# Nine of twelve convolution panels by seven block products, gated attention kept in DRAM meanwhile, and row tile loads held behind the first weights

## What is computed

```python
h = rms_norm(x, g_mix); z = h @ w_in
q, k, v, r, a_lr, c_b, c_c, c_x, g_a, g_b = split_columns(z)
o = gla_chunked(q, k, v, log_a)                 # 4 heads
o = rms_norm(o, g_gla) * silu(r)                # "gated attention"
y_a = o @ w_branch_a
y_conv = causal_dwconv(c_c * c_x, w_conv)       # 3 taps over positions
y_b = (c_b * y_conv) @ w_branch_b
mixed = sigmoid(g_a) * y_a + sigmoid(g_b) * y_b
x = x + mixed @ w_out
x = x + moe_ffn(rms_norm(x, g_ffn), ...)        # 4 of 32 experts for each token
return rms_norm(x, g_final)
```

## Time and profile before

| | us |
|---|---|
| median of three runs | 2480.02 (2477.66 to 2481.63) |
| profiled execution | 2477.27 |
| its span, first to last instruction | 2475.3 |
| TensorE busy | 2415.0 (98%) |
| VectorE busy | 1497.9 (61%) |
| ScalarE busy | 1220.5 (49%) |
| mean granted clock of TensorE | 0.992 |

### The profile page before, as it was taken

The page is one execution under the profiler, slowest core; times in us unless marked ns, Lnnn a source line. Parts: engine busy times, 40 slices in busy tenths (PEclk is TensorE's granted clock), DMA queues, the critical chain, the costliest instruction groups (busy, mean ns, idle before and its releaser), DMA issues.

```text
span 2475.3 us, 39936 instructions
## 1 busy us (share of the span) xinstructions
PE 2415.0 (98%) x13519; PEld 1920.0 (78%) x13520; DVE 1497.9 (61%) x1485; ACT 1220.5 (49%) x1232; POOL 371.8 (15%) x388
## 2 busy tenths in 40 slices
PE   7999999999999999997999999999999999999997
PEld 7888777788888888895778777777777887777775
DVE  4221333243323234347789887888877898788977
ACT  5522444321111121155677765676756776667766
POOL 0000000000000000534212211212121212212120
PEclk9999999999999999998999999999999999999998
DMA  4124232313422222537899998999989998989998
GB/s 134 35 37 66 69 72 69 65 43 51 51 52 51 97 90 85 182 130 273 280 378 380 327 347 267 363 330 362 328 281 324 376 380 304 320 304 377 348 341 305
DMA packets 258117, 536.96 MB, mean 217 GB/s; under 512 B 28824, under 2 KB 71576, under 8 KB 256928
## 3 DMA queue, kind: packets, MB, share of 16 engines
q1 hardware_dynamic: 237184, 489.35, 58.8%
q0 software_dynamic: 20864, 46.64, 6.9%
HBM read 493.32 MB, written 42.63 MB: 217 GB/s over the span
## 4 chain that ended last, share of the span: by engine, by line
PE 51%; DMA 1%; DVE 1%; issue 0%; SPq 0%; ACT 0%; POOLq 0%; DVEq 0%; ACTq 0%
PE m_y L2302 5%; PE m_gate L2304 5%; PE m_gate L2302 5%; PE m_lin L2302 5%; PE m_lin L2304 5%; PE m_gate L2303 5%; PE m_lin L2303 5%; PE m_y L2304 4%; PE m_y L2303 4%; PE m_spill L2341 4%; PE m_spill L2353 2%; PE m_turn L2286 1%; PE m_gate L2310 1%; PE m_y L2310 1%; PE m_lin L2310 1%; PE m_gate L2272 1%
## 5 line engine op out<-in xcount | busy, mean ns | idle before, releaser
L2110 DVE TENSOR_TENSOR m_w_lo<-raw,m_w_hi 128x2048 fp32r<-128x2048 f32 x382 | 867.2, 2288 | 204.4 <-ACT m_w_hi L1985 202.1
L1985 ACT CAST m_w_hi<-raw 128x2048 fp32r<-128x2048 f32 x382 | 730.9, 1913 | 353.2 <-PE m_lin L2304 243.4
L107 PE MATMUL c_bank<-h_hi_r,ring_hi 128*128 128x512 f32 x640 | 251.7, 393 | 0.9 <-PEq L417 0.9
L109 PE MATMUL c_bank<-h_lo_r,ring_hi 128*128 128x512 f32 x640 | 249.5, 390 | 0.0
L110 PE MATMUL c_bank<-h_hi_r,ring_raw_r 128*128 128x512 f32 x640 | 249.2, 389 | 0.0
L153 ACT CAST ring_hi<-ring_raw 128x2048 fp32r<-128x2048 f32 x43 | 82.2, 1911 | 316.0 <-DMA ring_raw<-in_w_in 143.9
L2302 PE MATMUL m_gate<-m_w_hi,x_hi 128*128 128x512 f32 x508 | 215.8, 425 | 0.0
L2302 PE MATMUL m_y<-m_w_hi,m_a_hi 128*128 128x512 f32 x512 | 211.0, 412 | 1.8 <-DVE m_a_lo L2162 1.8
L157 DVE TENSOR_TENSOR ring_raw_r<-ring_raw,ring_hi 128x2048 fp32r<-128x2048 f32 x43 | 99.1, 2305 | 180.7 <-ACT ring_hi L153 180.4
L2303 PE MATMUL m_y<-m_w_lo,m_a_hi 128*128 128x512 f32 x512 | 200.4, 391 | 0.0
L2304 PE MATMUL m_y<-m_w_hi,m_a_lo 128*128 128x512 f32 x512 | 200.4, 391 | 0.0
(11 more groups left out here) (389 smaller groups left out, 4242.0 us busy)
## 6 DMA issues: line engine op xcount, KB each, us to landing
raw<-in_w_gate_up SPq DMA_DIRECT2D x512, 512.0 KB, 11.5
raw<-in_w_down SPq DMA_DIRECT2D x256, 512.0 KB, 13.3
ring_raw<-in_w_in SPq DMA_DIRECT2D x31, 1024.0 KB, 9.3
gates<-work POOLq DMA_DIRECT2D x32, 256.0 KB, 3.7
work<-gates SPq DMA_DIRECT2D x8, 1024.0 KB, 7.5
v<-in_x SPq DMA_DIRECT2D x8, 512.0 KB, 13.6
ring_raw<-in_w_branch_b SPq DMA_DIRECT2D x4, 1024.0 KB, 5.3
ring_raw<-in_w_branch_a SPq DMA_DIRECT2D x4, 1024.0 KB, 5.2
```

Of the source, the lines that this page charges most:

```text
L107: pe.matmul(out, left_hi(k), right_hi(k), start=first and k == kts[0], stop=False, skip_group_check=True)
L109: pe.matmul(out, left_hi(k), right_lo(k), start=False, stop=False, skip_group_check=True)
L1985: act.copy(w_hi[:, p % WS].rearrange("p k b n -> p (k b n)"), raw[:, raw_slot(m)].rearrange("p k b n -> p (k b n)")).then_inc(signals.whi, 1)
L2110: dve.tensor_tensor(w_lo[:, p % WS].rearrange("p k b n -> p (k b n)"), raw[:, raw_slot(m)].rearrange("p k b n -> p (k b n)"), f32(w_hi[:, ...
```

## The change

**Seven products.** A panel is a product of 2 by 2 blocks: weights a11, a12, a21, a22 (channel block by half of the contraction) by activations h11 to h22 (half of the contraction by half of the tokens). Panels 20 to 22 stay as they are. Panels 23 to 31 (`FIRST_SEVEN`, z = 0 to 8) are computed by Strassen's method in Winograd's form: seven products of 4 slices of the contraction each, in place of eight. Per panel VectorE makes four sums of weight blocks (in place, in the raw slot), and each of the seven left operands ("forms", 512 elements) is split by itself: high by ScalarE (`form_high`), low by VectorE (`form_low`), into four slots in the high half of the ring, four products ahead; from the third form of the last panel on two slots and two products ahead (`last_use`, `forms_at`), since the other half of the ring takes panel 32. The sums of activations (T1 to T4) are made once, during panels 20 to 22, by VectorE passes of 2048 elements (`whole_of`, `made`) and split by both engines (`turned_hi`, `turned_lo`), the last of them behind form 3. The products of a panel go to three banks: 0 and 4 to the first, 1, 3 and 5 to the second, 2 and 6 to the third. Between them ScalarE copies product 0 away (`first_c`), and VectorE adds it to the banks (`sum_b`, `sum_c`), since later products go on in the same banks; `finish` adds up the result r and multiplies it as before. TensorE waits for `b_summed` before product 3, `first_kept` before 4, `read22` before 5 and `c_summed` before 6, and for `form_lo` before each. The taps of kind 1 are spread over products 5 and 6 and the first three of kind 2.

**Gated attention.** T2 and T3 lie in the buffer of `v`. So SP stores its eight row tiles to the DRAM tensor `o_rows` as they are finished and loads them back (`o_loaded`) once product 3 of the last panel is done.

**Loads of row tiles.** Row tile 2 waits until the first half of the first weight panel has landed, row tile 3 until the second has.

**Semaphores.** Those of the earlier stages are also cleared by GpSimd ahead of `join_branches`.

The diff, cut to its core:

```diff
+def last_use(m):
+    if m >= SEVEN * (SEVENS - 1) + 2:
+        return m - 2
+    return m - 4
 ...
+    def form(self, m):
+        z, f = divmod(m, SEVEN)
+        slot = (m + 2) % 4 if z < SEVENS - 1 else 2 + f % 2
+        both = self.hi[:, slot // 2].rearrange("p k n -> p (k n)")
+        here = both[:, slot % 2 * 4 * NP:(slot % 2 + 1) * 4 * NP]
+        hi, lo = (here[:, i * 2 * NP:(i + 1) * 2 * NP].rearrange("p (k n) -> p k n", n=P) for i in range(2))
+        return hi, lo
 ...
+                if i == 2:
+                    sp.wait_ge(first_loaded, 16)
+                if i == 3:
+                    sp.wait_ge(ring.loaded[0], 16)
                 sp.dma_start(xt[:, i], x[i * P:(i + 1) * P, :]).then_inc(x_loaded[i], 16)
 ...
+            def store_o(i):
+                sp.wait_ge(o_done, 2 * TT + 2 * (i + 1))
+                sp.dma_start(o_rows[:, i], v[:, i]).then_inc(o_stored, 16)
             for n in range(GATE + 2, END):
-                sp.wait_ge(ready, results(n - 1))
+                if n < FIRST_SEVEN + 2:
+                    sp.wait_ge(ready, results(n - 1))
+                else:
+                    sp.wait_ge(form_lo, SEVEN * (n - FIRST_SEVEN - 1))
 ...
+                if n == CONV:
+                    for i in range(TT - 1):
+                        store_o(i)
+                if n == CONV + 1:
+                    store_o(TT - 1)
             for n in range(2):
-                sp.wait_ge(ready, results(END + n - 1))
+                sp.wait_ge(form_lo, SEVEN * (SEVENS - 1 + n))
                 ring.load(sp, END + n, panel_view(w_branch_b)[:, :, n * NP:(n + 1) * NP])
+            sp.wait_ge(done, SEVEN * (SEVENS - 1) + 4)
+            for i in range(TT):
+                sp.dma_start(v[:, i], o_rows[:, i]).then_inc(signals.o_loaded, 16)
 ...
+            def form_high(m):
+                z, f = divmod(m, SEVEN)
+                n = FIRST_SEVEN + z
+                if m < 2:
+                    act.wait_ge(ready, results(n - 1))
+                elif m < 4:
+                    act.wait_ge(ready, results(n))
+                else:
+                    act.wait_ge(done, last_use(m) + 1)
+                act.wait_ge(ring.loaded[n % 2], 16 * (n // 2) + 16)
+                if f in (1, 2, 3, 6):
+                    act.wait_ge(summed, 4 * z + {1: 2, 2: 1, 3: 3, 6: 4}[f])
+                act.copy(ring.form(m)[0], ring.block(n, *((0, 0), (0, 0), (1, 0), (1, 0), (0, 1), (1, 1), (0, 1))[f])) \
+                    .then_inc(form_hi, 1)
 ...
+            act.wait_ge(o_done, 4 * TT)
+            turned_hi(0)
+            act.wait_ge(o_stored, 16 * TT)
+            turned_hi(1)
+            turned_hi(2)
+            form_high(0)
+            form_high(1)
+            act.wait_ge(ready, results(CONV + 3))
+            form_high(2)
+            form_high(3)
+            turned_hi(3)
+            for z in range(SEVENS):
+                c, kind = divmod(z + 3, 3)
+                bank = 4 * ((FIRST_SEVEN + z) % 2)
+                for f in range(SEVEN):
+                    m = SEVEN * z + f
+                    if f == 0:
+                        act.wait_ge(done, m + 1)
+                        if z:
+                            act.wait_ge(*taken_by(z - 1, 3))
+                        act.copy(first_c, banks[bank][:, :]).then_inc(first_kept, 1)
 ...
+                    for at_m in forms_at(z, f):
+                        form_high(at_m)
+                    if z == SEVENS - 1 and f == 0:
+                        act.sem_inc(ring.hi_ready, SEVENS)
+                        act.wait_ge(done, SEVEN * z)
+                        ring.split_hi(act, END)
 ...
+            def form_low(m):
+                z, f = divmod(m, SEVEN)
+                n = FIRST_SEVEN + z
+                a11, a12, a21, a22 = (ring.block(n, b, half) for b in range(2) for half in range(2))
+                hi, lo = ring.form(m)
+                dve.wait_ge(form_hi, m + 1)
+                dve.tensor_tensor(lo, (a11, a11, a21, a21, a12, a22, a12)[f], f32(hi), ALU.subtract) \
+                    .then_inc(form_lo, 1)
+                if f == 0:
+                    dve.tensor_tensor(a21, a21, a22, ALU.add).then_inc(summed, 1)
+                    dve.wait_ge(summed, 4 * z + 1)
+                    dve.wait_ge(form_lo, m + 1)
+                    dve.tensor_tensor(a11, a21, a11, ALU.subtract).then_inc(summed, 1)
+                if f == 2:
+                    dve.wait_ge(summed, 4 * z + 2)
+                    dve.wait_ge(form_lo, m + 1)
+                    dve.tensor_tensor(a21, a22, a11, ALU.subtract).then_inc(summed, 1)
+                if f == 4:
+                    dve.wait_ge(form_lo, m + 1)
+                    dve.tensor_tensor(a12, a12, a11, ALU.subtract).then_inc(summed, 1)
 ...
+            ring.split_lo(dve, CONV + 1)
+            whole_of(t_x, 0, 1)
+            whole_of(t_y, 0, 0)
+            made(t_y, t_x, t_y)
+            whole_of(t_z, 1, 1)
+            made(t_x, t_z, t_x)
+            made(t_z, t_z, t_y)
 ...
+                if r == 1:
+                    ring.split_lo(dve, CONV + 2)
 ...
+            turned_lo(0)
+            dve.wait_ge(t_lo, 1)
+            whole_of(t_y, 1, 0)
+            made(t_y, t_y, t_z)
+            turned_lo(1)
+            turned_lo(2)
+            dve.wait_ge(tap_done, 6)
+            for r in range(4):
+                dve.wait_ge(ready, results(CONV + 2) + r + 1)
+                dve.tensor_tensor(qk[:, r // 2, half_cols(r)], banks[r][:, :], qk[:, r // 2, half_cols(r)],
+                                  ALU.mult).then_inc(y_done, 1)
+            form_low(0)
+            form_low(1)
+            form_low(2)
+            form_low(3)
+            turned_lo(3)
+            for half in range(2):
+                dve.wait_ge(signals.gate_stored[half], 16 * GATES // 2)
 ...
+            def finish(z, r, bank, other, read, nth):
+                c, kind = divmod(z + 3, 3)
+                if kind == 0:
+                    dve.wait_ge(u_done, 4 * c)
+                    dve.tensor_tensor(cc[:, r // 2, half_cols(r)], bank, other, ALU.add).then_inc(read, 1)
+                    return
+                dve.tensor_tensor(other, bank, other, ALU.add).then_inc(read, 1)
+                dve.wait_ge(read, z + 1)
+                multiply(z, r, other)
+            def multiply(z, r, value):
+                c, kind = divmod(z + 3, 3)
+                if kind == 1:
+                    dve.wait_ge(tap_done, 6 * c)
+                    dve.tensor_tensor(u[:, r // 2, edge_cols(r)], value, cc[:, r // 2, half_cols(r)],
+                                      ALU.mult).then_inc(u_done, 1)
+                else:
+                    dve.wait_ge(tap_done, 6 * c + (3 if r // 2 else 6))
+                    y = qk[:, BPP * c + r // 2, half_cols(r)]
+                    dve.tensor_tensor(y, value, y, ALU.mult).then_inc(y_done, 1)
+            for z in range(SEVENS):
+                c, kind = divmod(z + 3, 3)
+                bank = 4 * ((FIRST_SEVEN + z) % 2)
+                p_a, p_b, p_c = (banks[bank + i][:, :] for i in range(3))
+                if z:
+                    b_free = taken_by(z - 1, 4) if kind != 1 else (read12, z)
+                for f in range(SEVEN):
+                    m = SEVEN * z + f
+                    if f:
+                        dve.wait_ge(done, m + 1)
+                    if f == 1:
+                        dve.wait_ge(first_kept, z + 1)
+                        if z:
+                            dve.wait_ge(*b_free)
+                        dve.tensor_tensor(sum_b, p_b, first_c, ALU.add).then_inc(b_summed, 1)
+                    if f == 2:
+                        if z:
+                            dve.wait_ge(*taken_by(z - 1, 1))
+                        dve.tensor_tensor(sum_c, p_c, first_c, ALU.add).then_inc(c_summed, 1)
+                    if f == 3:
+                        dve.wait_ge(c_summed, z + 1)
+                        if kind == 1:
+                            dve.wait_ge(read22, z)
+                        finish(z, 3, p_b, sum_c, read22, 1)
+                    if f == 4 and kind:
+                        if kind == 1:
+                            dve.wait_ge(cc_done, 4 + c)
+                        multiply(z, 0, p_a)
+                    if f == 5:
+                        finish(z, 2, p_b, first_c, read21, 3)
+                    if f == 6:
+                        dve.wait_ge(b_summed, z + 1)
+                        finish(z, 1, p_c, sum_b, read12, 4)
+                    for at_m in forms_at(z, f):
+                        form_low(at_m)
+                    if kind == 1 and f >= 5:
+                        if f == 5:
+                            dve.wait_ge(u_done, 4 * c + 3)
+                            tap(c, 0, 1, None, 0)
+                        else:
+                            tap(c, 1, 1, None, 1)
+                            tap(c, 2, 1, None, 2)
+                            dve.wait_ge(u_done, 4 * c + 4)
```

(49 more changed lines are left out.)

186 lines of the change are left out of this document (109 added, 77 removed).

## The result

| | before | after |
|---|---|---|
| median, us | 2480.82 (2477.66 to 2481.93, 4 runs) | **2460.22** (2459.69 to 2460.74, 4 runs) |
| profiled execution, us | 2477.27 | 2460.41 |
| its span, us | 2475.3 | 2458.7 |

The ratio is **0.9923, 95% interval 0.9911 to 0.9935**, 0.8% faster. The forecast was 2461.8. The two profiled executions lie 16.9 us apart, where I had 18.2; the one of before is at the low end of its runs, so the medians lie 20.6 apart.

The account below looks back on a forecast made before the run. TensorE, busy 2415.0 of 2475.3 us, was taken as the bound. The terms -24.5 + 7.0 + 1.9 - 2.6 = -18.2 us gave 2461.8 us by the median, range 2457 to 2471.

Parts of the forecast that it names:

- The walk of the nine panels: All 63 products of the seven-product panels, followed through each engine's instruction order and waits with durations from the old profile.
- 1: Nine convolution panels go from eight products to seven: 108 matmuls fewer at 0.2267 us each, -24.5 us.
- 2: VectorE and ScalarE fit in a seven-product panel; no product waits from the second to the eighth panel.
- rival (c): VectorE becomes the bound in kind-2 panels, slower than before: 2490 us, chance 0.03; something between, no change, 0.04.
- 3: First seven-product panel, no run-up: product 0 is 1.6 us late and product 3 2.7 late, +4.3 us.
- 4: Last seven-product panel, two slots left: form 4 is 1.2 us late and form 5 1.1 late, +2.3 us.
- 5: Change of stages behind the panels: VectorE ends 2.8 us after the matmuls instead of 0.9, +1.9 us (1 to 3).
- 6: Panels 20 to 22: added VectorE passes fit in idle time, o_rows stores delay panel 21's load; 0, at most +4 us.
- 7: The 4 MB reload delays gate loads behind the stage, 6 us of cover left: 0, at most +3 us.
- rival (b): Transfers come late, panel 21's load behind the stores or the gates behind the reload: +7 us, 2469, chance 0.12.
- 8: Kernel start: held row tiles remove a 1.5 us wait and raise the clock earlier, -2.6 us (-3.8 to +2).
- Rival (a): Waits in the seven-product stage drop TensorE's clock: +3 us, or +6 at both ends of the stage, 2468; chance 0.10.

Follow-up runs that it names:

- the repeated sums: Changed kernel, with control values bounded at zero in the experts' loop, VectorE making sum_b four times over in panels z = 1 to 7: 2473.33 us, ratio 0.9967.
- the one with GpSimd: Changed kernel, with control values bounded at zero in the experts' loop, four low splits of the last panel moved from VectorE to GpSimd: 2470.17 us, ratio 0.9958.

## Why the prediction was right

The walk of the nine panels, whose durations all came from the rows of before, is the part that held best: 15.6 us predicted (24.5 - 7.0 - 1.9), 15.6 measured.

- **1**: 108 matmuls at 0.2267 us, as the records show.
- **2**: no wait from the second to the eighth panel. VectorE's passes over narrow blocks take 0.69 us like the others (63 of L953, mean 688 ns), which was the open price of rival (c). No wait of TensorE falls between 637 and 784 us. The slack of 0.2 us ahead of product 3 of kind 2, and some 1.8 elsewhere, was confirmed from the other side by the repeated sums. At the durations of this kernel rival (c) has no place: 2.2 us more VectorE work ahead of product 3 brought only 0.5 to 2.2 us a panel.
- **3**: idle 1.47 and 2.46 us, 4.4 with the restarts (predicted 1.6 and 2.7). **4**: idle 1.18 and 0.85, 2.5 with the restarts (1.2 and 1.1). Together 7.0 predicted, 7.0 measured. But in the last panel I read the waits as costs of single passes in VectorE's way; the experiment with another order shows that they and the late end of the stage are one shortage, VectorE's 24.1 us.
- **5**: the gap from last to first matmul is 3.25 instead of 1.44 us, +1.8 (predicted +1.9).
- **6, 7**: no DMA ended a wait of TensorE here. The gates landed 14.3 us behind the first matmul of panel 32 and were wanted at 21.8 (estimated: 14, with 6 us of cover): rival (b) was empty in both its places. A late landing did cost 1.6 us, but in the routing, which no part of the sum covers. What I had not costed is the issue on SP, which had 2.7 us left.
- **8, mis-sized**: -2.6 predicted, -4.2 measured (-4.8 with the hold alone). Of it the wait is 1.7 (predicted 1.5); the clock gave the rest, some 2.5, where I took 1.1 and had 2.3 as the best case. That bound came from one number of before, "6.2 us after the last wait", which I moved with the wait. In after the matmuls became fast with the first ones behind the resumption, 4.7 us after 13.46. The 0.38 us that I read as the slow duration is that of a matmul which the change of the clock caught; the slow ones last 0.43.
- **Rival (a)** was right in part. I gave it 0.10 and placed it behind the wait at product 3, where it fell in one experiment (the repeated sums) but not in after. In after it came behind the wait of 2.86 at the change of stages, for 1.7 us.
- **Luck**: these 1.7 us and the 1.6 of the late landing are 3.3 us that I had at nothing, and the start gave 1.6 us more than I had. They partly cancel: -18.2 became -16.9. The range was also summed too narrowly: it took -1.5 as the bad end of the start, where part 8 has +2, and left out the +4 and +3 of parts 6 and 7.

## What to carry to other kernels

Where an instruction list without reordering feeds TensorE, walk it with durations from the rows: it placed five waits to 0.3 us here, and the changed versions of both ends to 0.4 and 0.1 (not the one with GpSimd, whose durations it had no rows for). Look at the first and last round of a pipeline, where there is no run-up or where the next stage's work stands in the list, and ask whether a wait there is order (then reorder) or an engine's total (then only less work helps). And cost a short wait of TensorE at itself plus a possible fall of the clock behind it, 1.7 us a time here.
